# Moving GpSimd's last two low parts of X from a stage's first weight pair into its second, between the sums and low parts of that pair's weights

## The reference, cut to what matters

```python
x = x + (g_a * (o @ w_attn_out) + g_b * ((h * gelu(yg)) @ w_lru_out)) @ w_o
gate, up = jnp.split(rms_norm(x, ffn_norm) @ w_gate_up, 2, axis=-1)
x = x + (jax.nn.silu(gate) * up) @ w_down
```

## Time and profile before

| what | value |
|---|---|
| median of 3 runs | 1718.15 us (1715.52 to 1721.18) |
| profiled execution, its own time | 1716.74 us |
| its span in the trace | 1714.9 us |
| TensorE matmul busy | 1642.5 us, 96% of the span |
| GpSimd busy | 1048.6 us, 61% |
| VectorE busy | 1042.1 us, 61% |
| ScalarE busy | 623.0 us, 36% |
| granted TensorE clock over the span | 0.986 |
| chain that ended last, by engine | PE 62%, POOL 10%, DMA 3%, DVE 2% |

### The profile page before, as it was taken

The page is one execution under the profiler, slowest core; times in us unless marked ns, Lnnn a source line. Parts: engine busy times, 40 slices in busy tenths (PEclk is TensorE's granted clock), DMA queues, the critical chain, the costliest instruction groups (busy, mean ns, idle before and its releaser), DMA issues.

```text
span 1714.9 us, 29333 instructions
## 1 busy us (share of the span) xinstructions
PE 1642.5 (96%) x11338; PEld 1555.8 (91%) x11338; DVE 1042.1 (61%) x1613; ACT 623.0 (36%) x1308; POOL 1048.6 (61%) x746
## 2 busy tenths in 40 slices
PE   6999999999999999989898998999999999999999
PEld 4999998988889898879797987999999999898999
DVE  5767673964746555647788878333333334859585
ACT  4354533233342434424223433333333333333332
POOL 4656552221223221388977838777777777989896
PEclk9999999999999999989999999999999999999999
DMA  4111113233213131255441511222233222373634
GB/s 164 38 62 61 61 49 105 67 79 106 60 60 97 67 90 66 97 189 187 152 151 71 181 56 63 83 95 79 75 129 124 84 78 76 113 277 108 257 122 168
DMA packets 72765, 182.13 MB, mean 106 GB/s; under 512 B 14704, under 2 KB 26416, under 8 KB 72000
## 3 DMA queue, kind: packets, MB, share of 16 engines
q1 hardware_dynamic: 51376, 159.13, 26.0%
q10 hardware_dynamic: 21264, 21.27, 4.2%
HBM read 131.36 MB, written 49.28 MB: 105 GB/s over the span
## 4 chain that ended last, share of the span: by engine, by line
PE 62%; POOL 10%; DMA 3%; DVE 2%; issue 2%; ACT 1%; SPq 0%; ACTq 0%; DVEq 0%
PE bank L585 60%; POOL xl L556 5%; POOL wsl L549 3%; POOL wsum L545 2%; PE bank L745 1%; DMA mb_scratch<-ev 1%; ACT xh L1175 1%; POOL praw L545 1%; DMA o_scratch<-ot 1%; DVE qstd L1422 1%; DMA spare<-mb_scratch 0%; DMA praw<-in_weights 0%; DVE pr L1473 0%; DVE xl L1502 0%; DVE qt L1436 0%
## 5 line engine op out<-in xcount | busy, mean ns | idle before, releaser
L585 PE MATMUL bank<-xh,wsh 128*128 128x264 f32 x2178 | 625.4, 287 | 31.3 <-POOL wsl L549 22.5
L585 PE MATMUL bank<-xh,wsl 128*128 128x264 f32 x2178 | 622.2, 286 | 0.0
L585 PE MATMUL bank<-xl,wsh 128*128 128x264 f32 x2178 | 621.8, 285 | 0.0
L585 PEld LDWEIGHTS bank<-xh,wsh 128*128 128x128 f32 x2178 | 413.5, 190 | 35.5 <-POOL wsl L549 28.3
L585 PEld LDWEIGHTS bank<-xl,wsh 128*128 128x128 f32 x2178 | 413.6, 190 | 0.0
L585 PEld LDWEIGHTS bank<-xh,wsl 128*128 128x128 f32 x2178 | 413.4, 190 | 0.0
L585 PE MATMUL bank<-acth,wh 128*128 128x352 f32 x1008 | 338.0, 335 | 8.8 <-issue 5.7
L585 PE MATMUL bank<-acth,wl 128*128 128x352 f32 x1008 | 328.3, 326 | 0.0
L585 PE MATMUL bank<-actl,wh 128*128 128x352 f32 x1008 | 327.0, 324 | 0.0
L499 POOL TENSOR_SCALAR wh<-wraw 128x512 fp32r<-128x512 f32 x104 | 85.0, 817 | 385.8 <-PE bank L585 375.6
L549 POOL TENSOR_TENSOR wsl<-praw,wsh 128x512 fp32r<-128x512 f32 (+1 forms) x158 | 236.8, 1499 | 87.3 <-ACT wsh L1158 87.1
(11 more groups left out here) (165 smaller groups left out, 2444.6 us busy)
## 6 DMA issues: line engine op xcount, KB each, us to landing
praw<-in_weights SPq DMA_DIRECT2D x34, 1024.0 KB, 4.9
wraw<-in_weights SPq DMA_DIRECT2D x52, 512.0 KB, 3.3
h_scratch<-ev SPq DMA_DIRECT2D x44, 264.0 KB, 2.1
acc<-h_scratch SPq DMA_DIRECT2D x4, 2112.0 KB, 13.2
ev<-x_scratch SPq DMA_DIRECT2D x6, 1056.0 KB, 5.1
spare<-x_scratch SPq DMA_DIRECT2D x6, 1056.0 KB, 4.9
praw<-in_weights SPq DMA_DIRECT2D x8, 768.0 KB, 5.1
x_scratch<-ev SPq DMA_DIRECT2D x5, 1056.0 KB, 4.0
```

The source lines that it names most:

```text
L585: return nc.tensor.matmul(*args, **kw)
```

## The change

Only GpSimd's list changes; no operation is added or dropped, and the lists of the other engines are the same row by row. GpSimd's parts 4 and 5 (5 and 4 in GATE_UP) leave the first pair. In the second pair sum 1 is held back behind low (f+1,1) and the first of the two parts; the second part follows low (f+1,2).

```diff
                 for r in range(PRODUCTS):
                     if r == 2 and p == X_FIRST[GATE_UP]:
                         part_low(t, 0)
-                    if r in (0, 1, 2):
+                    late = p == X_FIRST[t] + 1 and r == 1
+                    if r in (0, 1, 2) and not late:
                         w_sum(p, r)
-                    if r == 3 and p == X_FIRST[t] and t in (ATTN_OUT, DOWN, DOWN + 1, DOWN + 2):
-                        part_low(t, 4)
                     if r == 4:
                         w_sum(p, 3)
-                        if p == X_FIRST[t]:
-                            for k in POOL_LOWS[t][-2:]:
-                                if k == 5 or t in (LRU_OUT, OUT, GATE_UP):
-                                    part_low(t, k)
                     if not in_fp32(p, r):
                         w_low(p, r)
+                    if late:
+                        part_low(t, POOL_LOWS[t][-2])
+                        w_sum(p, r)
+                    if p == X_FIRST[t] + 1 and r == 2:
+                        part_low(t, POOL_LOWS[t][-1])
```

## The result

The changed kernel takes 1735.01 us (median of 4 runs, 1731.48 to 1736.11) against 1719.18 (4 runs, 1715.52 to 1721.18): the ratio is 1.0091, 95% interval 1.0068 to 1.0114. So it is 15.8 us slower. The forecast was 1752, 35 us slower, range 1726 to 1764: the sign holds, the size is less than half.

The account below looks back on a forecast made before the run. The prediction took the kernel as bound mostly by TensorE, with waits for GpSimd at a stage's second pair. Lateness 23.7, plus clock 15.9, less 4.2 absorbed, is +35.4 us on 1716.74: 1752 us, range 1726 to 1764.

Parts of the forecast that it names:

- Where the waits go: TensorE: gaps at (f+1,0) close; one of 4 to 7 us opens before (f+1,3), ended by a low part.
- 16 instructions instead of 12 behind the release: GpSimd, between the end of (f,2) and low (f+1,3): 16 instructions at 1.27 us, 20.3 us in stage 5.
- VectorE's turns: VectorE's two-SBUF-input instructions add their own time to GpSimd's stretch: 2.35 us wide, 0.65 short; 10.3 in stage 5.
- +23.7: Sum over seven stages of how much later (f+1,3) starts, from -2.3 us in stage 0 to +6.9 in stage 5.
- The test of the forecast: Stage 5 before, sum 3 to low (39,3): taking turns gives 22.9 to 24 us against 22.8 measured; overlap gives 15.2.
- The clock: TensorE behind each wait at (f+1,3): half clock costs 2.27 us in each of seven stages, +15.9 in all.
- what absorbs: At (6,0): the 2.60 us wait goes, and about 1.6 of slow clock with it, -4.2 us.
- The rule of the Trainium skill: VectorE with two SBUF inputs and GpSimd reading SBUF exclude each other for the whole instruction; PSUM bank reads do not count.
- Only the lateness, no clock: Rival: the gaps fall so that TensorE's clock holds; +20 us, 1736; chance 0.12.
- It only shifts the wait: Rival: the gap at (f+1,0) becomes one as long at (f+1,3), within 5 us of before; chance 0.05.
- VectorE's turns fall away: Rival: VectorE runs ahead while GpSimd idles, so GpSimd runs at 1.27 us; -18 us, 1699; chance 0.11.

Follow-up runs that it names:

- first_moved: Changed kernel, but only the first part (4; 5 in GATE_UP) moves, behind low (f+1,1); the second stays behind sum 3 of the first pair: 1732.24 us, ratio 1.0074.
- second_moved: Changed kernel, but only the second part (5; 4 in GATE_UP) moves, behind low (f+1,2); the first stays where it was before: 1717.76 us, ratio 0.9987.
- part3_twice: Changed kernel in which VectorE makes part 3 of X twice in each stage: 1748.35 us, ratio to before 1.0163.
- part3_lean: Changed kernel with VectorE's low part 3 cut to one of its four chunks in stages 1 to 6: 1724.92 us, ratio to before 1.0038.
- head_only: Changed kernel with both parts moved in stages 0 to 3 alone, at their old place in stages 4 to 6: 1717.84 us, ratio 0.9995.
- filled: Changed kernel with 28 extra matmuls (20 in stage 6) in TensorE's wait before (f+1,3): 1733.63 us, ratio to before 1.0104.
- down_filled: Changed kernel with both parts moved in stages 4 to 6 alone, plus 44, 44 and 28 extra matmuls in their waits before (f+1,3): 1733.04 us.

## Why the prediction came out too high

- **Where the waits go: right.** The waits at (1,0), (5,0) and (9,0) closed, one of 3.1 to 6.2 us stands before every (f+1,3), ended by a low part (L549), and in stage 0 there are two, 2.54 before (1,2) and 4.18. GpSimd idles 5 to 9 us before sum 3 in stages 1, 4, 5 and 6 (6.91, 5.17, 9.05, 7.41).
- **16 instructions instead of 12 behind the release: right**, and shown by first_moved against second_moved: with the first part moved there are 16 and the loss is 13 us, with the second part moved there are 12 and it is none.
- **VectorE's turns: the step that failed.** The forecast charged what VectorE's instruction takes alone, 2.35 and 0.65. GpSimd's instruction is held up by less, 2.14 and 0.48. The working had the row to read that from: 3.41 - 1.27. It also counted one or two short instructions too many a stage, and 1.27 for each instruction where they start 1.25 apart. In stage 5: 20.3 + 10.3 was forecast, 20.0 + 6.4 + 1.9 came. Stage 1 by the right prices: 20.0 + 4 x 2.14 + 7 x 0.48 = 31.9, and the trace has 31.3 (808.99 to 840.27), forecast 34.3. In stage 2 one whole wide instruction fell into the stretch and the end of another, not two, and the stretch began at 916.6, 922.0 on the axis of before, not at 923.8. In stage 3 it also began earlier than forecast: low (14,1) started at 1042.0, which is 1046.5 on the axis of before, and not 1048.0, since the wide instruction ahead of it had run beside an idle GpSimd (from 1039.94, 2.35 us) and was over. All this is the 14 us between +23.7 and +9.8. As an estimate, the two prices make some 8 of them, by the forecast's own counts: 20 wide at 0.21 and some 25 short at 0.17. That the turns exist and have about this size, part3_twice and part3_lean show in both directions. How many fall into the stretches is read from the trace; no run took that apart.
- **The test of the forecast that hid it.** The replay of stage 5 of before gave "22.9 to 24" against 22.8 measured, and was read as agreement. It was a lower end that already stood above the measurement, over 12 instructions, and it charged the third wide instruction half, although low (39,3) took 3.41 us beside it, the whole price. Counted in full the replay gives 24.2, 1.4 above the measurement; over 16 instructions and seven stages that became a good part of the error. "Taking turns fits" was true, but the price it fits is the lower one.
- **The clock: right**, 14.4 against 15.9, and **what absorbs: right**, 5.2 against 4.2, at (6,0) as named.
- **The rule of the Trainium skill** ("SBUF — State Buffer", section "Who interferes with whom": two such instructions exclude each other for the whole instruction) has the mechanism, and bank reads indeed add nothing: of part 5's four chunks in stage 5 only the one beside the wide instruction is stretched (3.42), and the one from 1597.26 took 1.31 beside three reads of a bank from 1597.19 to 1598.42. The partner's own time, which the forecast charged by it, is too high as a price, by a tenth for a wide instruction (2.35 against 2.14) and by a third for a short one (0.65 against 0.48): the measurement decides.
- **The rivals.** "Only the lateness, no clock" gave 1736, near the measured 1735, but for a wrong reason: the clock did fall, for 14 us, and the lateness was 10, not 24. The result alone would have favoured it; the windows rule it out. "It only shifts the wait" is true of stages 0 to 3 (head_only 0.9995), not of the DOWN stages. "VectorE's turns fall away" is ruled out by 9.36 and 7.24 us for four chunks.
- **The range** holds 1735 in part by luck: its low end stood for half the clock loss missing and 10 us of lateness, and what was missing was 14 us of lateness and next to nothing of the clock.

## What to carry to other kernels

Before you move work on an engine that waits, mark where it would have waited anyway: work taken out of such a slot, ahead of the release, comes back behind it (here 28.3 us instead of 22.8 in stage 5). Then look at what the engine will do in the place that the work leaves: here it idled 3.6 to 5.8 us in the DOWN stages when only the second part moved. Price a shared resource by how much longer the instruction that suffers gets in the trace, not by how long its partner takes alone; and if a replay of the old stretch comes out at or above its measurement, lower the price until it fits before multiplying it. Split such a change by part and by stage: here one half of it, in three stages, was a gain of 3.7 us inside a change that loses 15.8.

## What the runs showed that was not expected

- One VectorE instruction with two SBUF inputs took 14.57 us instead of 3.4 while GpSimd ran ten in a row, each at its undisturbed 1.25 to 1.32 us, and it ended one VectorE duration after the last of them. So the turns are not always taken one by one. It happened once in the twelve traces of this study; whether the runs of filled at 1742 to 1757 and of down_filled at 1741 and 1747, which have no trace, are the same event stays open, and so does what sets it off.
- A wait filled with matmuls of about its length (down_filled) kept the clock at the 2.4 GHz level. Of the waits filled for 3.5 us with idle time left behind the fill (filled), those of stages 1 and 3 kept it (2.83 and 1.88 us idle) and those of stages 4 and 5 did not (1.95 and 1.96).
- The same wait of 2.31 us before (35,0) was followed by a granted clock of 1.00 in one execution and of 0.50 in another, 1.5 us apart. One trace does not tell whether a wait of this length costs the clock.
